# Sums of squares of the DSA queries from rounded parts, new step orders, and a shorter weight stream in a two-layer decoder trunk

## The reference

```
def hybrid_layer(h, ...):
    a = rms_norm(h, attn_norm)
    proj = a @ w_in                       # dq dk dv iq iw ik fq fk fv ff gq gk gv gg glr
    dq = partial_rope(rms_norm(heads(dq, 4), dsa_q_norm), pos)
    dk = partial_rope(rms_norm(dk, dsa_k_norm), pos);  iq, ik = partial_rope(iq), partial_rope(ik)
    o_a = dsa_attention(dq, dk, dv, iq, iw, ik, k_top)      # the indexer picks 128 keys
    o_b = forgetting_attention(rms_norm(fq), rms_norm(fk), fv, log_f)
    o_c = rms_norm(gla_chunked(gq, gk, gv, log_a)) * silu(gg)
    h = h + concat(o_a, o_b, o_c) @ w_out
    f = rms_norm(h, ffn_norm)
    gate, up = jnp.split(f @ w_gate_up, 2, axis=-1)
    return h + (jax.nn.silu(gate) * up) @ w_down
```

## Time and profile before

| what | value |
|---|---|
| median of three runs | 1331.12 us |
| the profiled execution, its own time | 1330.2 us |
| its span, first to last instruction | 1328.4 us |
| PE busy | 1308.3 us, 98% |
| DVE, ACT, POOL busy | 644.7, 539.5, 550.2 us |
| granted TensorE clock | 1.000 |

### The profile page before, as it was taken

One profiled execution on the slowest core, in us unless ns is written; L12 is line 12 of the kernel. 1 busy time (PEld: TensorE's weight loads), 2 busy tenths in 40 slices (PEclk: granted clock), 3 DMA queues, 4 the chain that ended last, 5 costly groups with the idle time before them and its releaser, 6 DMA issues.

```text
span 1328.4 us, 22871 instructions
## 1 busy us (share of the span) xinstructions
PE 1308.3 (98%) x8670; PEld 1195.7 (90%) x8670; DVE 644.7 (49%) x1084; ACT 539.5 (41%) x874; POOL 550.2 (41%) x274
## 2 busy tenths in 40 slices
PE   7999999999999999999999899999999999999998
PEld 7989999999999999999998899887878888888887
DVE  4698888563333333322226999985643333331000
ACT  4575548543222222322234665485332222222221
POOL 3553313243444444444445453212444444444445
PEclk9999999999999999999999999999999999999999
DMA  5322110132222222233323221101222222223334
GB/s 186 93 68 68 62 49 33 42 102 92 83 95 88 85 95 93 81 99 106 96 79 100 79 82 55 43 31 48 95 89 92 92 92 95 93 94 105 101 99 154
DMA packets 33595, 114.11 MB, mean 86 GB/s; under 512 B 4352, under 2 KB 4736, under 8 KB 33536
## 3 DMA queue, kind: packets, MB, share of 16 engines
q1 hardware_dynamic: 32816, 112.23, 25.5%
q10 hardware_dynamic: 720, 1.09, 0.2%
HBM read 109.84 MB, written 2.10 MB: 84 GB/s over the span
## 4 chain that ended last, share of the span: by engine, by line
PE 53%; issue 31%; POOL 9%; DVE 4%; ACT 1%; DMA 0%; POOLq 0%; SPq 0%; ACTq 0%; DVEq 0%
PE ps L740 20%; PE ps L746 10%; POOL wlo L621 9%; PE ps L831 5%; PE ps L832 5%; PE ps L837 5%; PE ps L961 1%; PE ps L909 1%; PE ps L934 1%; PE ps L944 1%; DVE score L1609 1%; PE ps L1018 1%; PE ps L797 1%; PE ps L1000 1%; PE ps L1030 1%
## 5 line engine op out<-in xcount | busy, mean ns | idle before, releaser
L621 POOL TENSOR_TENSOR wlo<-raw,whi 128x1024 fp32r<-128x1024 f32 x202 | 496.8, 2461 | 723.4 <-ACT whi L1140 723.0
L1140 ACT ACTIVATE whi<-raw 128x1024 fp32r<-128x1024 f32 x202 | 214.0, 1059 | 586.1 <-PE ps L746 545.8
L740 PE MATMUL ps<-xhi,whi 128*128 128x264 f32 (+1 forms) x1096 | 327.8, 322 | 7.0 <-ACT whi L1140 6.9
L740 PE MATMUL ps<-xlo,whi 128*128 128x264 f32 (+1 forms) x1096 | 326.4, 322 | 0.0
L740 PEld LDWEIGHTS ps<-xhi,whi 128*128 128x128 f32 x1096 | 207.0, 189 | 24.7 <-ACT whi L1140 6.7
L740 PEld LDWEIGHTS ps<-xlo,whi 128*128 128x128 f32 x1096 | 206.7, 189 | 15.9
L746 PE MATMUL ps<-xhi,wlo 128*128 128x264 f32 (+1 forms) x1096 | 195.4, 322 | 0.3 <-POOL wlo L621 0.2
L746 PEld LDWEIGHTS ps<-xhi,wlo 128*128 128x128 f32 x1096 | 162.9, 188 | 17.3 <-issue 1.0
L831 PE MATMUL ps<-xhi,whi 128*128 128x264 f32 (+1 forms) x632 | 177.7, 310 | 0.0
L832 PE MATMUL ps<-xlo,whi 128*128 128x264 f32 (+1 forms) x632 | 171.4, 300 | 0.0
L740 PE MATMUL ps<-hlo,whi 128*128 128x264 f32 (+1 forms) x528 | 157.3, 321 | 0.0
(11 more groups left out here) (204 smaller groups left out, 1714.6 us busy)
## 6 DMA issues: line engine op xcount, KB each, us to landing
raw<-in_weights SPq DMA_DIRECT2D x202, 512.0 KB, 3.4
out_hT<-h SPq DMA_DIRECT2D x8, 256.0 KB, 4.0
...
xnb<-feat SPq DMA_DIRECT2D x20, 33.2 KB, 2.0
feat<-xnb SPq DMA_DIRECT2D x20, 33.2 KB, 2.0
...
```

The source lines that it names most:

```text
L621: nc.gpsimd.tensor_tensor(wlo[:, b], raw[:, b], whi[:, b].bitcast(F32), ALU.subtract).then_inc(split_done, 1)
L740: nc.tensor.matmul(bank(bank_no, cut.stop - cut.start), whi[:, b, k % KT], x(k)[t][:, cut], start=(first and k == ks[0] and t == 0), stop= ...
L1140: return nc.scalar.activation(whi[:, b], raw[:, b], ACT.Copy).then_inc(hi_done, 1)
```

## The change

1. DQ and DQ + 1 join `SPLIT_SQUARES`. In each layer ACT writes two more squares and POOL runs two more subtractions, and the two norms are formed from rounded parts.
2. `STEPS_OF` and `BANKS_OF` are replaced for both layers.
3. The first rounding of the FFN loop (unit `U_GU + 2`) now stands ahead of the load of silu's table, and each later one stands at the end of the loop's body instead of at the next body's start. The loop so rounds one down unit as well, ahead of the load of the other table.
4. The stream ends with the last weights: SP, ACT and POOL leave out the two unused units.
5. The last DVE addition is made in two halves of 256 tokens, and each half has its own store.

```diff
-STREAM = DEPTH * UNITS + 2
+STREAM = DEPTH * UNITS
...
-SPLIT_SQUARES = (FQ, FQ + 1, FK, FK + 1, GV, GV + 1, GV + 2, GV + 3)
+SPLIT_SQUARES = (DQ, DQ + 1, FQ, FQ + 1, FK, FK + 1, GV, GV + 1, GV + 2, GV + 3)
...
-     POOLE: "AAQQAAAAACACACAQQACAQAAAAAQAAAAACCACAC",
+     POOLE: "AAQAQAACAACACACCAACAAQQQAAAQAAAAACCCACAA",
...
                 first = l * UNITS + N_PROJ + 4
-                last = (l + 1) * UNITS + 4 if l < DEPTH - 1 else STREAM
+                last = (l + 1) * UNITS + 4 if l < DEPTH - 1 else DEPTH * UNITS
...
             for k in range(KT):
                 sp.wait_ge(layer[-1].acc_free, 2 + N_OUT + MF + k + 1)
-                sp.dma_start(out[k * 128:(k + 1) * 128, :], h[:, k, META:META + SEQ]).then_inc(stored, 16)
-            sp.wait_ge(stored, 16 * KT)
+                if k < KT - 1:
+                    sp.dma_start(out[k * 128:(k + 1) * 128, :], h[:, k, META:META + SEQ]).then_inc(stored, 16)
+
+            rows, half = slice((KT - 1) * 128, KT * 128), SEQ // 2
+            sp.dma_start(out[rows, 0:half], h[:, KT - 1, META:META + half]).then_inc(stored, 16)
+            sp.wait_ge(layer[-1].acc_free, 2 + N_OUT + MF + KT + 1)
+            sp.dma_start(out[rows, half:], h[:, KT - 1, META + half:META + SEQ]).then_inc(stored, 16)
+            sp.wait_ge(stored, 16 * (KT + 1))
...
-                with pool.Fori(N_PROJ // 2 + 1, UNITS // 2 + 1) as j:
+
+                with pool.Fori(N_PROJ // 2 + 1, UNITS // 2 + (1 if l < DEPTH - 1 else 0)) as j:
...
                 prenorm(1)
+                round_unit(U_GU + 2, 0)
                 nc.scalar.preload_act_table_set("silu_and_others")
                 with act.Fori(0, MF // 2) as j:
                     for b in range(2):
-                        round_unit(j * 4 + (U_GU + 2 * b + 2), 0)
                         act.wait_ge(ev.gate_scaled, j * 2 + (b + 1))
...
+                        round_unit(j * 4 + (U_GU + 2 * b + 4), 0)
+
                 nc.scalar.preload_act_table_set("natural_log_exp_and_others")
...
                     for s in range(3):
-                        round_unit(U_DN + 3 * m + s + 2, (3 * m + s) % 2)
+                        if m + s and (l < DEPTH - 1 or U_DN + 3 * m + s + 2 < UNITS):
+                            round_unit(U_DN + 3 * m + s + 2, (3 * m + s) % 2)
...
                     dve.wait_ge(half_done, half0 + 2 * (U_DN + 3 * (m + 1)))
+                    if l == DEPTH - 1 and m == KT - 1:
+                        for a in (0, SEQ // 2):
+                            of = slice(META + a, META + a + SEQ // 2)
+                            nc.vector.tensor_tensor(h[:, m, of], wide(l, 2 * (m % 2))[:, a:a + SEQ // 2], h[:, m, of],
+                                                    ALU.add).then_inc(ev.acc_free, 1)
+                        continue
```

More of the change, by code:

```diff
@@ L217 @@
 STEPS_OF = (
-    {PE: "AAABAAAAAADAAAAAAAAAAAAAFAAAAAALAAAAAAAAADAMAMAADAMAMAMMAAMMFMMADAAAAAAAAADAAAAPPAAXXAAXAADAAXALAAaA"
-        "ALbAAdAADAAAAAXXXAXXAXAaXAYXAYAbMXAMaAdAMAAAMZYZAXYXZAYXZYXbAAdAAAAZYXZAZAYXALPZAAARRAAPLAYXAYXMAaMa"
-        "bAAAdLZZYAXYXZZbYXYAdZYAZZXXYXAAYLXATSARSAaAATRATRASSATTaZbYXAdZDZYXYXAADZYXZbYAdADZAYaAAZDYZAAXXZXb"
-        "AYdXAYXAAaAZYXZYXZYXZbYadZYZYZfZbfdfff",
-     ACTE: "BACDAAAPLAHHICIDAMMCIIDMAMCMMMMMMDJACOADIICJPPIIAPXXDAXXLJaALCeDAJXXXXXXAXaYYXMMaeXAMMYYXYXYePAYXXKY"
-          "AXXLPAPLYXYMaXaMALeYYXXYXeYYYXXXLAXTYaTAUTTTCYaXeDCXYXYDCAYXeDCYYUDYaAXXXeYUXXYaAYUXYXVYXYVVVYeYae",
-     DVEE: "AAADAAAAFAAPAAHHIIADAMMIIADMMAMMMMFNDANANANOADIIANIIAXXXANNXNADNNANNcNANNNADNNANXXXPXXXAXePXMMcMMXAA"
-          "NNANNXXPcPXXAAeePAXXANNNANRRNNAXMMXMNMcANNeAXNXcXNeNNXXXANXNNSSARNANRNNRSSANUNcXNeNXDXNANDcXNeNDANNU"
-          "DAXXXcXeAXUAXUXVVXWcVVWWWece",
-     POOLE: "AAQAQAAAACACAQQCAAACAQAAAQAAAAACCCACAA",
-     DMAE: "AEEAEAGAAEAEAGAAAAAAAAAAAAAAAAA"},
@@ L229 @@
-    {PE: "AAAAAABAAADAAAAAAAAAFLAAAAADAAMMAMADAMMAMAFMMAAADMMAAAAADAAAAADAAAAAAXXXAAAYYXAAMMaAMADMAAAAALLAAAXA"
-        "PAAPAAAAZYZYXXAZYXAAAaAAAAAZYXbALAZYXZAAYXZYXZbYXAAMAaARRALMAPPALAAAAAALASTSARATRASTSdRATZYXTZYXZAYX"
-        "ZYbXdADadZZAYYXADXZYZbXAYXZYXaZYXZDZYAYXdbXZYXZaZYYdXZbXYdZXYaZXYZXZYXYbDZYZYZaZdbfdffff",
-     ACTE: "BACADAALPACIIHIDHMMAMCIDAMCMMAMMDMMCIIAJDCIIOADCJAXXXYYJXMaMMADMJALLAPXAPPYYXYXXAaAYPLYXYXYYKXXMaXAL"
-          "MPPALALTUTATeTYUXYTAXYCYeXXDeaCYYUDYXXAYXCaYYXXDXYYUXYXaeYYeXXYeXAaXYYXCVXYYXDYVYVaVee",
-     DVEE: "AAADAAAFPAIIHIADMHMMIADMNMAMFMMANDAIINANDNAIINAODAXXXNANXMMMMANNNNDANNNNNANNNANXNANNANNXXPXAPAPAPcXA"
-          "NXPXXMMXMAARRNNMANNNANNANNNSNSRANNRUNSNRSceANXNUXNNXXceNNDAXeNUXDcXNXNXNXNDAXcXUVXVeVXecXeXXXWXcDVWW"
-          "Wece",
-     POOLE: "AAQQAAAAACACACAQQACAQAAAAAQAAAAACCACAC",
-     DMAE: "AAEEEAGAAEAEAGAAAAAAAAAAAAAAAAA"},
+    {PE: "AAABAAAAAADAAAAAAAAAAAAAFAAAAAALAAAAAAAAAAADAMAAMAADMMAAAMPMADMAMAFAADAAAAMMAADPAAAAAAXAAXAAALAAAALA"
+        "XXAAAaADbAAAAAAdAAAAAAXXXAXXAXAXaAYXAbMYXAdMZaZAYAXZYAXZbAYXAdAYZAXZAAYAXZAAYAXZAAYAXARRAAPYXALLALMA"
+        "MMAaPaAAMbLATSdSZYZAXTZYXYXZYXbRSaZZTdYAXYXZYZXbYXSAaRARTTZdYXZYXZDYXZbAYAdaADZZYYAAZDZAAAADAAAAAbXX"
+        "AXAYXYAAdXZZaYYZXZbXYYXdZYZaYZZbfdffff",
+     ACTE: "BACDAAAPLAHHCIIADMCIIMADMMCMPMDMMCJADJCMMAODIIPAPXXJALIIALCXXaDAePJAXXXAXXXXYaXMYXeMAYaYKXXXYeYAXYXY"
+          "AXYXAPYLLLMMMXPaaAMLTeYXTYYYXXXaTYeYXXXYYXaAUTTCYeYXXDCXYYeaDCYYDCAUDUAXXXYYXUXYYAeaVVXVYXeYXYaYVe",
+     DVEE: "AAADAAAAFAAPAAHAHIAIDMAIIMADMMMNAMDNFADAMMNNANNNOIAAIXDXANANNNAIINXXANPAPPAcPADNANNNXXXAXXNXXANXMcXM"
+          "AMMPXXAcXNNANXNANXNANXNAeXeeNRARNXNNANMNMMANNMcNSSAXeNNXXXcRSNNXXeXNXSRAcRNNUNXXeNXDcNNAeNDNNADNAUNA"
+          "DNXXAXUXcAXUVVVVeXWXcWXeWWce",
+     POOLE: "AAQAQAACACACCACAQAQAACAQAAAQAAAAACCCCAAA",
+     DMAE: "AEEAEAGAAAEAEGAAAAAAAAAAAAAAAAA"},
@@ new lines @@
+    {PE: "AAABAAAAADAAAAAAAAAFAAAALAAPAAAMMADMAMMAMAMMAMMADAAAAADAFAAADAAAAADAAAALAAAXXAXADYYAXALMAMAAMMAPAAAA"
+        "XAAAAAZYXAAaZYXZYAAXZYbXAAZYZXYaZXAYZbPXAYARARaAALAPAAALMAMXdAAAZYZYLZYAZXXdbXAYAAAaAZYZYLZXATRZYSSX"
+        "XbAYXXdATRZYSTSXRZYZYTTXXdZYaADbaAdZDYZAYADAZAXXADXAAYXZYbXdZYXZZYaYZbXdZYXZYfYaZZbfdfff",
+     ACTE: "BACDAAAPLAHHIIPCIIMAMMDAMMCMMMAMMDCADCJDCAJDIIJAIILCXXXAYYDOALMMJXMAMPPXYXAAaYYPYXXYXaYYKXXYXPAaLPAL"
+          "MMeXYALYYeXXXYaYALYXTYXXYeXXATUYTXYYTTCeXaYXCaDeDCYYADUCAUDXXXAYYUYeXXaYVYVXVeVYXXYYae",
+     DVEE: "AADAAAFAAPHHIIAIMIAMMDMMMAMMNNDANANNNDAFADNNANNDIAINNIIXXXAANNNXDMAMONMMANNNNANXPPPXAAAPXNXXcPXXANXM"
+          "MRANRANNNANNAMXceNANNNXXeXNANcNAMNXNNRNXXSSXXeAcNRNSUSXRNNNXXNeNcNNDeDNANNDNAXXUXUDAXcXUVeVVVXWcWXWe"
+          "WXce",
+     POOLE: "AAQAQAACAACACACCAACAAQQQAAAQAAAAACCCACAA",
+     DMAE: "AEEAEAGAAAEAAEAGAAAAAAAAAAAAAAA"},
@@ L239 @@
 )
 BANKS_OF = (
-    "0202023023012302320202301303020301301301023102300201210212013202020201230203203013201302130310101300"
-    "20201202301201230320121203020230203013020301232",
-    "0202201203201300320201230123010202010320132013023013203020202020201310201301130130312031031201031230"
-    "12320320120202301130130101302032013",
+    "0202023023013023020120230201203201201201210212022002002222222220201202020203020230120230120210201231"
+    "32102302020123121023010310202013013121032030123",
+    "0202023023201320102020230130302302023012301203102320232022020201230201320132030201023231202012012012"
@@ L246 @@
+    "02301220120202020013103130013013012",
 )
```

## The result

The changed kernel took 1334.1 us (median of 13 executions, 1330.2 to 1337.1), the kernel before on the same chip 1330.9 us (13 executions, 1330.4 to 1331.5). The ratio is 1.0021 with a 95% interval of 1.0013 to 1.0029: 3.2 us slower, clear of the noise, though far less than 2%. The forecast was 1327.2 us, with 1323.4 to 1331.2 as its range.

A forecast was written before the change was run, and what follows sets the result against it. PE was taken as the bound, busy 1308.3 of 1328.4 us. Gains of 1.6 (norms), 0.9 (table load), 0.4 (end) and 1.0 (orders) sum to 3.9 us, predicting 1327.2 us, range 1323.4 to 1331.2.

The forecast's parts named there:

- The edits: FFN starts and program end: rounding ahead of the table load gains 0.9 us, halved last store 0.4 us.
- The new orders: Mixers of both layers: reordered steps gain 1.0 us of PE's waits, bounds a gain of 4.5 and loss of 7.3.
- the cover of the split squares: DSA query norms: PE's pieces between two norms hide the added ACT squares and POOL subtractions, put at 0 us.
- The cheaper norms: DSA query norms on PE: four products take 0.66 us instead of 1.06, gaining 4 x 0.40 = 1.6 us.
- 1.82 us in each of four: Four new norm chains: if each ends with PE idle for 1.82 us, the loss is 7.3 us; that rival had 8%.
- The 1.8 us above, less 0.8 for new waits: Mixers: the wait removed before FK's norm, less an allowance for new waits such as at the rotation, gains 1.0 us.
- The 1.82 us wait: Second layer, PE before FK's norm at 755.06: disappears because splits waiting for the DSA-query DMA stand behind that norm.
- The orders give the gain back: Rival, 28%: edits bring 2.9 us, but the longer `sq_parts` chain makes new waits of 0 to 3 us; 1329.7 us.
- Slower, by POOL's subtractions in DVE's way: Rival, 8%: four added POOL subtractions stop DVE instructions reading two SBUF operands; loss 7.3 us less 2.9, giving 1335.5 us.
- The test that I set for being wrong: Forecast is wrong if PE's waits in the two mixers add up to over 10 us.
- the other one: Forecast is wrong if DVE's score instructions beside POOL's subtractions stretch and PE waits over 1 us each at norms or `rope(1)`.

The follow-up runs named there:

- first experiment: Changed kernel with step orders, banks and plain DSA-query squares of the kernel before; moved rounding, shorter stream and halved last store remain: 1328.89 us, ratio 0.9987.
- fifth experiment: Changed kernel with its new orders and edits, but plain DSA-query squares and without POOL's first two subtractions of each layer: 1332.21 us, ratio 1.0012.
- sixth experiment: Kernel before with one PE wait added in layer one, ahead of the FFN's last products, until the whole hidden table is written: 1334.62 us, ratio 1.0030.
- the seventh: Kernel before with a PE wait added in layer one's down units until the hidden table's remainders are ready too: 1337.71 us, ratio 1.0053.
- the second: Changed kernel with all edits and split squares but orders and banks of before, POOL's added subtractions behind its fifth and sixth splits: 1332.91 us, ratio 1.0020.
- the twelfth: Old orders, all edits and split squares (as in the second), with five norms moved one or two product groups later on PE alone: 1340.80 us, ratio 1.0073.

## Why the prediction was wrong

The experiments take the sum apart, each part against its own runs of before. The edits were to give 1.3 us and gave 1.8. The new orders on top of them were to give 1.0 and cost 3.1 (first and fifth experiment). The split squares on top of both were to give 1.6 and cost 1.9 (fifth experiment and the changed kernel; these two intervals overlap). That makes 3.2 us slower in place of 3.9 us faster. Three steps failed: the cover of the split squares was taken as given, PE's waits were to shrink by 1.0 us and grew, and each wait was priced at its own length, with nothing for the clock.

**The edits (forecast 0.9 + 0.4 = 1.3 us): right.** The first experiment measured 1.8 us, and the ratio's interval of 0.5 to 2.9 us holds the forecast. The parts read off the profiles are 0.42 us at layer two's FFN start (forecast 0.4), 0.7 us at layer one's (forecast 0.6, and 0.9 taken for both together) and 0.7 us at the end (forecast 0.4), 1.8 us in all. Layer one's is read against the first experiment: from PE's low pass to its next product 4.10 us (307.22 - 303.12) in place of 4.36 (307.57 - 303.21), and from there to the next low pass 1.96 us in place of 2.38. At the end a half store landed in 1.8 us and not 2.25. Silu came 0.5 us later (forecast 0.4): 2.37 us after DVE's `sg` began, where it was 1.84 (967.41 - 965.57). PE did not wait for it.

**The cheaper norms (forecast 1.6 us): the products right, the cover wrong.** They read 0.66 us where nothing waited. "By itself I put this at 0; what covers it is PE's pieces between two norms" is the step that failed. In the old orders the cover was not there, and the longer chain cost 6.0 us of waits in four places. I had that price beside me as the first thing to fear (1.82 us in each of four) and gave it 8%, because I took the new orders to hide it. They do: the sum of waits for `sq_parts` is back at 2.8 us. But then the gain from the orders should have been set against the old orders with split squares, not the old orders as they were. Comparing the fifth experiment with the changed kernel, the split is worth nothing.

**The new orders (forecast 1.0 us): wrong in sign.** "The 1.8 us above, less 0.8 for new waits" is the step that failed. Between the first and the last product PE's waits grew from 9.6 to 12.6 us. The 1.82 us wait went, as I said, and `rope(1)` in layer two became a wait, as I feared (1.9 us against 0.8 us allowed). I did not foresee the waits of 2.8, 3.1 and 1.7 us. By the rows above the first two come from POOL splits beside DVE instructions with two SBUF inputs, 2.46 us in place of 0.37, the very rows I had read in the earlier trace rows. I held that effect against the added subtractions alone. It is where the steady splits fall in the new order that decides, and POOL has 200 of them. The Trainium skill (SBUF — State Buffer, "SBUF: two separate sides") describes the port pair that DVE and GpSimd share as an exclusive lock for a whole instruction. These rows agree: DVE's 2.46 us ends 0.17 us after POOL's split does. How much of the 3.1 us is longer waits and how much is the clock behind them the runs do not separate: the fifth experiment has no execution above 0.997.

**What was missing altogether: the clock.** Over the executions the sum without it is 1328.7 us, so the steps above miss by 1.5 us. The other 5.4 us up to 1334.1 are, by the same line, the granted clock. No term and no rival had it: each wait was priced at its own length. The sixth experiment shows a price near twice the length (3.8 us for 2.0), the seventh one and a half times (6.9 for 4.8). The kernel before has waits too, but few and short: none over 1.8 us behind the first product. That one was followed by the half level in the profiled execution of the first experiment (0.79 over 752 to 760 us, below), though not in that of the kernel before:

```profile
752.00:760.00 8.00, 6.17 (x39) 5.99 (x38) 6.04 (x12) 7.80 (x13) 3.46 (x2) 0.79 0.18 67
```

Why some executions of the changed kernel go down to 0.994 (16 us at the half level in all) and others only to 0.999 stays open, since the profiles caught only the 0.999 and the 0.997. In the fourteen profiles (two of the changed kernel, one of every other) each fall between the first and the last product begins behind a wait of PE of 1.2 us or more, or in the last part of one. The reverse does not hold: no fall followed the 2.4 us of the fifth experiment, the 1.93 and 1.95 us of the second or the 2.75 us of the twelfth. What decides between them stays open.

**The rivals.** "The orders give the gain back" had part of the mechanism at 1329.7 us, and is near what the line gives at full clock (1328.7). "Slower, by POOL's subtractions in DVE's way" ended nearest to the median, but by another way: POOL does stand in DVE's way, with its steady splits, while the waits are there without the added subtractions too (fifth experiment), and the clock is missing. The test that I set for being wrong, over 10 us of waits in the mixers, was met: 22.5 - 6.8 - 3.1 = 12.6 us against 9.6. So was the other one in its second half: PE waits 2.8 us at a norm and 1.9 us at `rope(1)`.
